# Long convolution: the filter's magnitude tiles added on GpSimd ahead of the norm's products

## What is computed

```python
def hyena_filters(T, w1, b1, w2, b2, w3, b3, w4, freq):
    ...
    filt = (hdn @ w4.astype(F32)).reshape(T, 2, D_INNER)
    ...
    filt = filt * jnp.exp(-t * deltas[None, :])[:, None, :]
    filt = filt / (jnp.sum(jnp.abs(filt), axis=(0, 1), keepdims=True) + HY_FILTER_EPS)
    return filt[:, 0], filt[:, 1]

def bidir_long_conv(v, h_fwd, h_bwd, skip):
    ...
    y = jnp.fft.irfft(jnp.fft.rfft(vf, n=n, axis=1) * jnp.fft.rfft(taps, n=n, axis=0)[None],
                      n=n, axis=1)[:, :T]
    return (y + vf * skip.astype(F32)).astype(v.dtype)
```

## Time and profile before

| | |
|---|---|
| median of three runs | 2439.29 us |
| profiled execution | 2438.29 us, span 2436.5 us |
| busy: TensorE, VectorE, ScalarE, GpSimd | 92%, 56%, 42%, 25% |
| mean granted clock of TensorE | 0.965 |
| the norm's products (L1032) | 192 rows in the trace, 440.7 to 715.1 us, a weight load of 128x128 each |

### The profile page before, as it was taken

One profiled execution on the slowest core, in us unless ns is written; L12 is line 12 of the kernel. 1 busy time (PEld: TensorE's weight loads), 2 busy tenths in 40 slices (PEclk: granted clock), 3 DMA queues, 4 the chain that ended last, 5 costly groups with the idle time before them and its releaser, 6 DMA issues.

```text
span 2436.5 us, 36864 instructions
## 1 busy us (share of the span) xinstructions
PE 2251.7 (92%) x15337; PEld 1857.1 (76%) x15337; DVE 1365.3 (56%) x2343; ACT 1012.2 (42%) x1844; POOL 612.1 (25%) x475
## 2 busy tenths in 40 slices
PE   7999998789899989999999988989988999699998
PEld 7999998789889988999899877866676667333332
DVE  4454544777873376666666667589555655411112
ACT  4344433444442355555555653344533432211112
POOL 2112113455542122222222211203121111133331
PEclk9999999799999999999999989999988999799999
DMA  5323421101015222222222223312341134699993
GB/s 179 105 70 98 133 87 36 34 20 36 18 31 143 78 62 73 80 75 70 66 80 65 71 60 82 103 35 70 79 118 48 53 100 139 241 365 379 369 375 153
DMA packets 225616, 272.79 MB, mean 112 GB/s; under 512 B 41112, under 2 KB 193657, under 8 KB 212778
## 3 DMA queue, kind: packets, MB, share of 16 engines
q1 hardware_dynamic: 211050, 259.90, 33.4%
q0 software_dynamic: 13824, 8.44, 1.2%
q10 hardware_dynamic: 576, 2.10, 0.2%
HBM read 303.19 MB, written 23.13 MB: 134 GB/s over the span
## 4 chain that ended last, share of the span: by engine, by line
PE 66%; DVE 20%; ACT 8%; POOL 3%; issue 2%; DMA 1%; SPq 0%; ACTq 0%; DVEq 0%; POOLq 0%
PE ps L93 15%; PE ps L94 14%; PE ps L95 14%; PE ps L4014 7%; PE ps L4057 4%; DVE prods L1168 2%; PE ps L1844 2%; DVE fsum L995 2%; ACT sp L115 1%; DVE wlo L103 1%; ACT whi L99 1%; DVE p L2139 1%; PE ps L3984 1%; PE ps L3130 1%; PE ps L2997 1%
## 5 line engine op out<-in xcount | busy, mean ns | idle before, releaser
L93 PE MATMUL ps<-hn_h,whi 128*128 128x264 f32 (+2 forms) x2256 | 689.5, 306 | 24.1 <-POOL wlo L103 9.9
L95 PE MATMUL ps<-hn_h,wlo 128*128 128x264 f32 (+2 forms) x2256 | 670.0, 297 | 0.0
L94 PE MATMUL ps<-hn_l,whi 128*128 128x264 f32 (+2 forms) x2256 | 669.5, 297 | 0.0
L93 PEld LDWEIGHTS ps<-hn_h,whi 128*128 128x128 f32 x2256 | 428.8, 190 | 53.8 <-issue 18.1
L95 PEld LDWEIGHTS ps<-hn_h,wlo 128*128 128x128 f32 x2256 | 427.5, 190 | 11.5
L94 PEld LDWEIGHTS ps<-hn_l,whi 128*128 128x128 f32 x2256 | 429.3, 190 | 9.0 <-issue 0.2
L103 POOL TENSOR_TENSOR wlo<-wraw,whi 128x2048 fp32r<-128x2048 f32 (+1 forms) x44 | 158.6, 3603 | 503.8 <-ACT whi L99 503.8
L99 ACT ACTIVATE whi<-wraw 128x2048 fp32r<-128x2048 f32 (+1 forms) x134 | 202.4, 1511 | 44.9 <-PE ps L95 38.1
L103 DVE TENSOR_TENSOR wlo<-wraw,whi 128x2048 fp32r<-128x2048 f32 (+1 forms) x90 | 172.0, 1912 | 48.9 <-ACT whi L99 48.8
L4014 PE MATMUL ps<-ex_raw,xT 128*64 128x512 f32 x600 | 135.4, 595 | 0.0
L755 DVE SCALAR_TENSOR_TENSOR c<-ub,vec,c 128x528 f32<-128x528 f32 x48 | 45.6, 950 | 128.5 <-ACT c L115 128.5
(11 more groups left out here) (696 smaller groups left out, 5384.0 us busy)
## 6 DMA issues: line engine op xcount, KB each, us to landing
ex_raw<-in_w_gate_up SPq DMA_DIRECT2D x49, 1024.0 KB, 8.1
wraw<-in_hy_w_in SPq DMA_DIRECT2D x32, 1024.0 KB, 5.7
wraw<-in_da_w_in SPq DMA_DIRECT2D x64, 512.0 KB, 4.3
ex_raw<-in_w_down SPq DMA_DIRECT2D x26, 1024.0 KB, 8.0
wraw<-in_w_gate_up SPq DMA_DIRECT2D x15, 1024.0 KB, 7.7
wraw<-in_w_in SPq DMA_DIRECT2D x14, 1024.0 KB, 5.5
wraw<-in_hy_w_out SPq DMA_DIRECT2D x8, 1024.0 KB, 7.5
wraw<-in_da_w_out SPq DMA_DIRECT2D x8, 1024.0 KB, 7.8
```

What stands on the lines that cost most here:

```text
L93: e.matmul(out, lhsT=l[0], rhs=r[0], start=start, stop=False)
L94: e.matmul(out, lhsT=l[0], rhs=r[1], start=False, stop=False)
L95: return e.matmul(out, lhsT=l[1], rhs=r[0], start=False, stop=stop)
```

## The change

A new function for GpSimd, `gpsimd_total`, waits until `dec` is complete, adds tile 1 to tile 0 (128x512), adds the first 9 rows of tile 2 to those of tile 0 (9x512), and adds the second direction to the first (128x256), each into `dec` in place and each after the event of the one before. `tensor_filter_end` now waits for the last of these and makes two products with ones, one for each half of the channels. GpSimd calls `gpsimd_total(0)` at the start, between `gpsimd_w4(1)` and `matrix(4)`, and `gpsimd_total(c+1)` at each turn, after `gpsimd_w4(c+2)` and ahead of `gpsimd_back(c, 0)`. Nothing else changes.

```diff
--- before.py
+++ after.py
@@ -1021,16 +1021,21 @@
             w.wait_ge("hy.vec", "hdn")
         act(e, abs0[0:n], hp[0:n, 0, :], ACT.Abs).then_inc(*mark("cv.act", "abs0", c, i))
 
+    def gpsimd_total(e, w, c):
+
+        w.wait_ge("cv.vec", "ab", c, 2)
+        flat = [dec[0:9 if i == 2 else 128, i].rearrange("p s c -> p (s c)") for i in range(3)]
+        e.tensor_tensor(flat[0], flat[0], flat[1], ALU.add).then_inc(*mark("cv.pool", "both", c))
+        w.wait_ge("cv.pool", "both", c)
+        e.tensor_tensor(flat[0][0:9], flat[0][0:9], flat[2], ALU.add).then_inc(*mark("cv.pool", "all", c))
+        w.wait_ge("cv.pool", "all", c)
+        e.tensor_tensor(dec[:, 0, 0], dec[:, 0, 0], dec[:, 0, 1], ALU.add).then_inc(*mark("cv.pool", "total", c))
+
     def tensor_filter_end(e, w, c):
         w.wait_ge("cv.vec", "vT", c, 0)
-        w.wait_ge("wf")
-        once = wf[:, 5:6]
+        w.wait_ge("cv.pool", "total", c)
         for h in range(2):
-            for i in range(3):
-                w.wait_ge("cv.vec", "ab", c, i)
-                for s in range(2):
-                    t = e.matmul(vb[0][:, h:h + 1], lhsT=dec[:, i, s, 128 * h:128 * h + 128], rhs=once if i == 2 else ones[:, 0:1],
-                                 start=(i == 0 and s == 0), stop=(i == 2 and s == 1))
+            t = e.matmul(vb[0][:, h:h + 1], lhsT=dec[:, 0, 0, 128 * h:128 * h + 128], rhs=ones[:, 0:1], start=True, stop=True)
         t.then_inc(*mark("cv.pe", "norm", c))
 
     def vector_filter_end(e, w, c):
@@ -1420,6 +1425,7 @@
         matrix(2)
         matrix(3)
         gpsimd_w4(e, w, 1)
+        gpsimd_total(e, w, 0)
         matrix(4)
         matrix(5)
         w.wait_ge("cv.pool", "mats", 5)
@@ -1431,6 +1437,8 @@
                 gpsimd_freq(e, w, c, z)
             if c < 6:
                 gpsimd_w4(e, w, c + 2)
+            if c < 7:
+                gpsimd_total(e, w, c + 1)
             gpsimd_back(e, w, c, 0)
             gpsimd_back(e, w, c, 1)
```

## The result

The changed kernel takes 2469.14 us (median of 6 runs, 2465.68 to 2472.61) against 2440.36 us for the kernel before in the same comparison: a ratio of 1.0117, 95% interval 1.0102 to 1.0133. The profiled execution has a span of 2466.9 us, 30.4 more than before.

The account below looks back on a forecast made before the run. The prediction took GpSimd's chain to `yl` as critical around each turn, with slack on TensorE. Six turns at +5.0, start -1.6 and last turn +1 gave +29.4, said as 2469 us; range 2453 to 2482.

Parts of the forecast that it names:

- The adds: GpSimd's three adds behind `w4l` at block 2's turn: 2.24, 1.7 and 0.7 us, with handoffs 4.76 us.
- the second rival: GpSimd and VectorE take turns for whole instructions; adds end 1.1 us later than forecast, six times: 2475 us, chance 0.2.
- TensorE and the norm: At a turn TensorE idles 7 to 8 us for the adds, then makes four norm passes at half clock, 0.99 us.
- The load and behind it: SyncE's `dec` load after the norm: 5.2 us to VectorE's product, 1.97 more to the spectrum product; +4.7 a turn.
- GpSimd's path to `yl`: At a turn, `y` and `yl` behind the adds take 6.8 us, ending at 533.9: +3.2, no longer last.
- A turn: Each of six turns, blocks 1 to 6, gets 5.0 us longer, bounds +2.8 and +6.3; together +30.
- the TensorE path: At a turn, 32 products to the filter's spectrum, then `hc`, behind the norm: +5.3 if all run at 1.2 GHz.
- The load path: At a turn, norm end through the next block's `dec` load to the spectrum product: 535.35 against 530.67, +4.7 us.
- The clock rival: TensorE stays at 1.2 GHz through a block's second spectrum pair, +6.1 a turn, 2475; through the third, 2498; chance 0.13.
- The start: Before the first block, GpSimd adds at once and the norm ends at 444.4 against 445.99: -1.6, bounds -3.1 and -0.5.
- The last turn: Block 7's turn, without `w4l` before or `dec` behind; adds end near 717.1: +1 us, bounds 0 and +2.5.
- The sum: Over the whole kernel, 30 - 1.6 + 1 = +29.4 us on the profiled 2438.29, said as 2469 us.

Follow-up runs that it names:

- experiment 3: Kernel before, with two norm products over one magnitude tile in place of twelve and no adds: 2436.77 us, ratio 0.9982.
- 7: Kernel before, with the second half's gating product `y` on VectorE instead of GpSimd, no adds: 2428.04 us, ratio 0.9956.
- experiment 1: Changed kernel, with TensorE's two norm products moved behind the new block's first two spectra at every turn: 2466.15 us, ratio 1.0099 to the kernel before.
- experiment 2: Changed kernel, with GpSimd's adds placed ahead of `w4l` at the turns: 2464.05 us, ratio 1.0088 to the kernel before.

## Why the prediction was right

- *What bounds the kernel before.* At its turns `yl`, not TensorE: experiment 3 (turn unchanged without the products) and 7 (turn shorter with a shorter way to `yl`) show it.
- *The adds.* Sizes 2.24, 1.7 and 0.7 were said; 1.72, 2.12 and 1.07 came. End of `w4l` to end of the last add: 4.85 said, 5.05 measured. The mechanism was that of the second rival, turns: each of the stretches is a wait until an operation of the other engine has ended, as the pair of timelines shows, and the trace agrees with the rule of the Trainium skill ("SBUF — State Buffer", "Who interferes with whom"). My price for that rival had been 5.95, because I let the first skip term delay the start by 0.5 and the third add wait for a whole skip term; in the run both waits were shorter. So the rival's mechanism held with nearly the forecast's price.
- *TensorE and the norm.* 0.99 us for four passes at half clock was said; 0.98 to 1.00 came. Idle 8.01 us, "7 to 8" was said.
- *The load and behind it.* Norm end to VectorE's product 5.2 said, 5.15 measured (529.73 to 534.88); from there 1.97 said and 1.97 measured. GpSimd's path to `yl`, 3.2 over the old value, was to lie 1.5 below the load's; it ended at 535.26, 1.6 below 536.85.
- *A turn.* +5.0 was said, +4.51 measured. I gave the TensorE path half its weight, for the low clock. It decided one turn of six, by 0.65 us: experiment 1 removed most of that path's lateness and 0.54 a turn came back. The load path alone, +4.7 in my working, was the better value: from a block's fifth product to the next block's first the mean went from 16.90 to 21.63, +4.73. Some 0.28 of it comes back behind the turn, where VectorE no longer meets the folds (0.42 in place of 0.70 for L1174's operation), which I had not counted.
- *The clock rival.* It asked for a low clock through the second pair of spectra. At block 2's turn the clock was back at about 534, after 21 of the 32 products of the first pair. TensorE ended that pair at 535.67, but `hc` started at 536.14, behind the magnitude that waits for the decay: the load hid the low clock. It didn't hide it at block 3's turn (0.65 us) and at the last one, where no load stands behind the norm.
- *The start.* -1.6 said, -2.68 measured: the adds took 3.8 us in place of 4.8, where VectorE's operations beside them are short (four of 128x342, 4.12 us together), and the norm 0.61 in place of 0.99, since the granted clock was 1.00 there and not 0.50. The bounds held it.
- *The last turn.* This is the step that failed: +1 said, +2.37 measured, near the upper bound. I let the adds take 4.8 us; they took 6.7, since the first was kept out by both halves of `fl_l`. And I took the cover to hold nearly, that is `yl` to end the turn as before; it ended on TensorE's 28 products at half clock, 0.99 us behind `yl`, which I had allowed for in the upper bound alone. Experiment 1 gives 0.82 of it back.
- *The sum.* 30 - 1.6 + 1 = 29.4 was said; 27.0 - 2.7 + 2.4 = 26.7 came, and 3.7 more arose after that. Of these 0.9 fell within block 7 and 2.8 later. The part of the kernel after the fifth product of block 7 took 1698.5 us before and 1701.3 after, and between 1698.2 and 1704.7 in the experiments with no edit there. So the nearness of 2469 to 2469.14 is in part luck: a turn said 0.5 too long and this spread cancel; what causes the spread was not tried.

## What to carry to other kernels

Work on an engine with slack is not worth removing by work on the engine that ends the critical chain, even if the new work is three operations for ten: here the ten were free and the three were not, and they cost twice over, by GpSimd's own time (3.5 us a turn) and by the load that hung on their result (1 us more). At one turn in six and at the last, TensorE's own late start at half clock was the longer path. Before adding a wait, list what the waited-for result releases (here a buffer, a load and the next block's first step) and follow that to the end; the stall that the profile shows on the waiting engine may be the cheapest part of it, as at most turns here. And ask which single operation on the critical engine another engine could do in its idle time: one such move gave 0.4%.

## What the runs showed of the hardware that I had not expected

A GpSimd operation that waits for VectorE's two-input work doesn't always get in after one operation. At the last turn of the changed kernel and in experiment 2 the first add was asked for during the first half of `fl_l` and started after the second: 3.32 us for an operation that takes 1.29 alone. Elsewhere GpSimd was let in between two such operations. VectorE's timeline of the changed kernel shows the pair of `fsum` beside a GpSimd operation and, later, alone:

```profile
550.02 2.39 DVE L995 TENSOR_TENSOR fsum<-hp 128x512 f32<-128x512 f32 x2
...
557.22 1.29 DVE L995 TENSOR_TENSOR fsum<-hp 41x512 f32<-41x512 f32 x2
```

The first pair took 1.1 us more. It has more rows than the second, 128 against 41, but that hardly counts: VectorE's L1001 takes 0.68 us with 128 rows and 0.67 with 41. GpSimd's operation begun at 550.12 took 1.73 us, so it ended at 551.85, inside the pair: it ran between the two parts. What decides between the two outcomes was not tried.

At the seven turns of the changed kernel the granted clock went to 0.50 while TensorE was idle, and stood there for 6.8 to 10.2 us in all. At block 2's turn that was about 524 to 534, though TensorE was fed without a gap from 528.72 on.
